# The last differential-attention steps of a hybrid encoder layer: another order of projection, map transposes, key tiles and value products

## The chip, the cores and the metric

The kernel runs on one core of a Trainium2 chip. The metric is the device time in microseconds; three runs of the kernel before gave 828.14, 828.20 and 828.29 us. The engines are named as the profile names them: PE (matmuls and transposes), DVE (vector), ACT (activation functions and copies), POOL, and SP, which issues most of the loads. Each works through its own list of instructions in order and waits on semaphores that the others raise.

## What is computed

One encoder layer on 1024 positions of width 1024: a norm, one wide input projection, two branches over head groups (gated linear attention, then differential attention), an output projection, cross-attention into 256 memory tokens, a last norm. The part that matters here:

```python
# differential attention, per head h and block of 128 queries
s = einsum('bhmqd,bhmkd->bhmqk', qb, kh) * scale     # two maps m, block-causal
p = softmax(where(allowed, s, -inf), axis=-1)
a = p[:, :, 0] - lam * p[:, :, 1]
o = einsum('bhqk,bhke->bhqe', a, vh)                 # then a head norm and a gate
mixed = concatenate([o_gla, o_diff], axis=-1)
x = x + mixed @ w_out
# cross-attention: keys and values of the memory tokens
kv = mem_n @ w_ckv                                   # K is its left half, V its right half
```

## The kernel before

Every float32 product is made of three matmuls of split operands (`_hi` and `_lo`: a rounded part that ACT writes, and the rest that DVE writes), lines 1849 to 1851. So each tile that PE produces and consumes again costs ACT a copy and DVE a subtraction (line 1386) before PE may use it.

The program is one list of stages (`stages()`), which every engine walks in the same order; each engine issues only its own part of a stage. Differential attention has 32 steps i (4 heads of 8 query blocks; step i looks at i % 8 + 1 key blocks of 128). The stages of a step:

- `proja`, `proj` (number 16 + i): the input projection of one block, 24 matmuls of 512 columns; `proja` is its first half where it is split, with other work between the halves.
- `TQK`: queries and keys transposed on PE (L2104), copied by ACT, their low part written by DVE (`qkT_lo`).
- `S`: scores (L2121, L2126). `max`: row maxima by DVE (L1648). `E`: two exponentials by ACT (L1270). `comb`: the two maps combined by DVE (L1656 to L1663); in step 31 in two pieces.
- `T`: the combined map transposed (L1921), in groups of up to four blocks; ACT writes `prT_hi`, DVE `prT_lo`.
- `PV`: the map times the values (L2144, L2146); DVE sums the halves (L1669), ACT squares them (L1101).
- `pvvar`, `pvfin`: variance, POOL's power, and the gated norm (L1675, L991, L1685).

Beside them: `MT`, a stored tile of mixed outputs brought back and transposed on PE (L1921, from `tile_a`); `K` c, a tile of cross-attention keys (24 matmuls of 256 columns), with `Ke` its copy and low part (`ck_hi`, `ck_lo`) into SBUF; `Ka`, the first 18 matmuls of `K` 0; and `("w", n)`, a weight tile split into `w_hi` (ACT) and `w_lo` (DVE), whose slot must have been given up by an older weight tile, and whose stage makes SP load tile n + 4.

Waits that matter below. `PV` of step i waits until the transposed map's low part is there and for a count of `qkT_lo` tiles (`tq_dve`). `MT` waits until all earlier transposed tiles but those of the other bank have been split (`turned_out`). Key tiles 0, 1 and 2 all use bank 0, so each waits for the `ck_lo` of the one before; key tiles 3 and 4 use banks 2 and 3, which belong to the scores, and tile 3 waits for the exponentials of step 31 (`s_act`). Key tile 0 needs the weight tiles 56 to 63.

Of the kernel before, what the change touches and what calls it, by code (L numbers as in the profile page):

```python
# [32 lines left out]
P = 128  # L33
# [77 lines left out]
def stages():  # L111
# [50 lines left out]
    n_turned = 0  # L162
    plan.extend([("S", 0), ("max", 0), ("E", 0), ("comb", 0)])
    plan.extend([("proja", GLA_STEPS + 2), ("TQK", 1), ("proj", GLA_STEPS + 2)])
    for i in range(last):
        plan.append(("S", i + 1))
        plan.append(("max", i + 1))
        plan.extend([("pvvar", i - 1)] if i else [])
        plan.extend(turned_maps(i))
        split = GLA_STEPS + i + 3 in PROJ_SPLIT  # L170
        if i + 2 < DIFF_STEPS and not split:
            plan.append(("TQK", i + 2))
        plan.extend([("pvfin", i - 1)] if i else [])
        plan.extend([("E", i + 1), ("comb", i + 1)])
        plan.extend([("loadm", 0, 0), ("loadm", 1, 0)] if i == DIFF_STEPS - TT - 4 else [])
        if split:
            plan.extend([("proja", GLA_STEPS + i + 3), ("TQK", i + 2)])
        if i + 3 < DIFF_STEPS:
            if i + 3 > DIFF_STEPS - TT and not split:
                plan.append(("proja", GLA_STEPS + i + 3))  # L180
                plan.extend(turned_tile(n_turned))
                n_turned += 1
            plan.append(("proj", GLA_STEPS + i + 3))
            if i + 3 > DIFF_STEPS - TT and split:
                plan.extend(turned_tile(n_turned))
                n_turned += 1
        if i == last - 2:
            plan.extend([("Ka", 0), ("PV", i), ("K", 0), ("Ke", 0)])
        elif i == last - 1:
            plan.extend([("K", 1), ("Ke", 1), ("PV", i)])  # L190
        else:
            plan.append(("PV", i))
    plan.extend([*turned_maps(last), ("pvvar", last - 1), ("K", 2), ("pvfin", last - 1), ("Ke", 2)])
    plan.extend(turned_tile(n_turned))
    n_turned += 1
    plan.extend([("K", 3), ("Ke", 3), *turned_tile(n_turned), ("PV", last), ("pvvar", last), ("pvfin", last)])
    n_turned += 1
    fill = [[("K", c), ("Ke", c)] for c in range(4, 8)] + [[("V", g, m)] for g in range(2) for m in range(MT)]
    for n, more in enumerate(fill):
        plan.extend(more)  # L200
        if n_turned < 2 * TT:
# [116 lines left out]
def with_weights(plan):  # L318
# [20 lines left out]
    for g in range(2, len(use)):  # L339
        before = use[g - 1]  # L340
        early = NW - KT
        for k in range(NK[g]):
            if use[g][0][0] == "X":
                p = use[g][0][1]
                if p == 0:
                    where = ("V", 1, 0) if k < 2 else ("MT", TT - 1, 1)
                else:
                    where = ("X", p - 1, (k // 2 + 1) if p == 1 else (k + 1) // 2)
                after.setdefault(where, []).append(("w", W0[g] + k))
                continue  # L350
            if use[g][0][0] == "Y" and use[g][0][1]:
                p = use[g][0][1]
                if p == 1:
                    where = ("Qe", 1, XH - 1, 0) if k == 0 else (("O", 1, XH - 2, 1) if k < 3 else ("Y", 0, 2))
                else:
                    where = ("Y", *divmod(4 * p + k - min(p + 4, 8), 4))
                after.setdefault(where, []).append(("w", W0[g] + k))
                continue
            if before[0][0] == "X":
                where = ("X", 5, 3) if k < 2 else ("X", 6, k // 2 - 1)  # L360
                after.setdefault(where, []).append(("w", W0[g] + k))
                continue
            where = before[(k + 1) * len(before) // (early + 1)] if k < early and len(before) > 4 else (
                before[min(k // 2, len(before) - 2)] if k < early else before[-1])
            if before[0] == ("K", 0) and k < early:
                where = ("Ke", 1) if k == 0 else ("T", DIFF_STEPS - 1, 1)
            if before[-1] == ("Q", 0, XH - 1, 1) and k >= early:
                where = ("PT", 0, XH - 2, 1)
            if before[0] == ("V", 0, 0) and k < 3:
                where = ("MT", 4, 1)  # L370
            if where == ("proj", GLA_STEPS + DIFF_STEPS - 2):
                where = before[-3]
            elif where == ("proj", GLA_STEPS + DIFF_STEPS - 1):
                where = ("E", DIFF_STEPS - 3) if k == early else ("TQK", DIFF_STEPS - 1)
            elif k >= early and where[0] == "proj" and GLA_STEPS < where[1] < GLA_STEPS + DIFF_STEPS - 1:
                i = where[1] - GLA_STEPS - 3
                where = ("PV", i) if k == early else ("T", i + 1, (i + 1) % TT // 4)
                after.setdefault(where, []).append(("w", W0[g] + k))
                continue
            after.setdefault(behind(where), []).append(("w", W0[g] + k))  # L380
# [65 lines left out]
def late_banks():  # L446
# [10 lines left out]
            bank[("Y", p, t)] = (*PJ_BANKS, 4, 5)[(4 * p + t + 2) % 6]  # L457
    before, held = {}, {}
    for stage in PLAN:
        if stage[0] in ("Ka", "Qa"):  # L460
            stage = (stage[0][0], *stage[1:])
        if stage in PJ and stage not in before:
            before[stage] = held.get(bank[stage])
            held[bank[stage]] = stage
# [47 lines left out]
def build(nc, a, out):  # L512

    with ExitStack() as ctx:
# [1331 lines left out]
        def _(pe):  # L1846
# [77 lines left out]
            for stage in PLAN:  # L1924
# [165 lines left out]
                elif kind == "TQK":  # L2090
# [1 line left out]
                    pe.wait_ge(pj_dve, GLA_STEPS + i + 1)  # L2092
                    wait(pe, tq_dve, i)
                    if TQK_BANK[i] == 1:
                        wait(pe, pv_sum, i - 2)
                    elif i >= 2:
                        turned_out(TR[("T", i - 2, 0)])
                    if i == 0:
# [30 lines left out]
                elif kind == "T":  # L2129
                    i, g = w  # L2130
                    pe.wait_ge(s_dve, i + 1 + (g if i == DIFF_STEPS - 1 else 0))
                    if g:
                        pe.wait_ge(tq_dve, i + 2 if i + 1 < DIFF_STEPS else DIFF_STEPS)
                    turn(stage, [prob[:, 0, cols(b)] for b in range(4 * g, min(4 * g + 4, i % TT + 1))])
                elif kind == "PV":
                    i = w[0]
                    t = i % TT
                    pe.wait_ge(ring_dve, TURN_ACT[("T", i, t // 4)] + 1)
                    wait(pe, pv_sum, i)
                    pe.wait_ge(tq_dve, min(i + 3, DIFF_STEPS))  # L2140

                    for b in range(t + 1):
                        v = (i - t + b) % NV
# [1 line left out]
                                  start=b == 0, stop=False)  # L2145
                        last = pe.matmul(bank1[:, 0:P], prT_lo[:, b, :], dv2[:, v, 0, :], start=False, stop=b == t)  # L2146
                    last.then_inc(pv_pe, 1)
                elif kind == "Ka":
                    job = ("K", *w)
                    pe.wait_ge(pj_dve, GLA_STEPS + DIFF_STEPS)  # L2150
                    project(job, late_bank(job)[:, 0:M], weights(P * w[0]), memory_tokens(slice(0, M)), 0, 6)
                elif kind == "K":
                    open_already = ("Ka", *w) in NTH
                    ps = banks[LATE_BANK[stage]] if open_already else late_bank(stage)
                    if w[0] == 3:
                        pe.wait_ge(s_act, DIFF_STEPS)
                    last = project(stage, ps[:, 0:M], weights(P * (w[0] % 4)), memory_tokens(slice(0, M)),
                                   6 if open_already else 0)
                    signal(last, stage, pr_pe)
                elif kind == "V":  # L2160
                    if LATE_BANK[stage] == 1:
# [98 lines left out]
```

## Time and profile before

| | |
|---|---|
| three runs | 828.14, 828.20, 828.29 us |
| the profiled execution's own time | 828.41 us |
| its span, first to last instruction | 826.7 us |
| granted clock of PE, mean | 0.998 |
| PE, DVE, ACT busy | 99%, 71%, 53% of the span |
| chain that ended last, share of PE | 92% |
| steps of differential attention in the span | about 203 to 488 us |
| the stretch that the change touches | about 399 to 491 us |

The span is 1.7 us shorter than the execution's own time. The busy time of PE counts each matmul until its result is out, while the next one has started already: a 512-column matmul is shown 0.39 us long and the next starts 0.23 us after it. So the busy share hides short pauses; the timeline's starts show them.

### The profile page before, as it was taken

The numbers are of one execution on the slowest core, as the hardware profiler recorded it, in microseconds if no ns is written. First come the engines' busy times: TensorE is split into PE (matmuls) and PEld (weight loads), VectorE is DVE, ScalarE is ACT, GpSimd is POOL, SyncE is SP. The second block draws the span as 40 slices with busy tenths as digits, with TensorE's granted clock in tenths as the row PEclk, the third lists the DMA queues.
The fourth block names the chain that finished last, engine by engine and source line by source line (L and its number), as shares of the span: only waits on it lengthen the run. The fifth ranks groups of instructions, "written<-read, shape, count | busy, mean of one in ns | idle before, by whom it ended". The sixth has DMA issues, their size and how long they took to land.

```text
span 826.7 us, 13231 instructions
## 1 busy us (share of the span) xinstructions
PE 814.4 (99%) x4586; PEld 683.9 (83%) x4586; DVE 586.1 (71%) x1360; ACT 435.6 (53%) x1057; POOL 83.7 (10%) x123
## 2 busy tenths in 40 slices
PE   8999999999999999999999999999999999999996
PEld 7888888888788888888888898888888888888885
DVE  6788677776578678767857878599835464367997
ACT  6875445454455345435545676544645454366443
POOL 3100121210010011111100000010010000001201
PEclk9999999999999999999999999999999999999999
DMA  8321359962233345645412268855422121206945
GB/s 289 115 83 39 102 179 199 186 132 66 62 108 109 88 79 108 130 86 116 102 61 84 61 211 262 265 148 128 134 96 72 45 65 43 85 13 139 215 93 203
DMA packets 70409, 99.21 MB, mean 120 GB/s; under 512 B 6596, under 2 KB 38472, under 8 KB 70344
## 3 DMA queue, kind: packets, MB, share of 16 engines
q1 hardware_dynamic: 52360, 64.29, 24.4%
q0 software_dynamic: 15392, 29.36, 19.8%
q10 hardware_dynamic: 2592, 4.72, 1.8%
q8 instruction: 37, 0.61, 0.3%
q14 instruction: 28, 0.23, 0.1%
HBM read 83.68 MB, written 31.46 MB: 139 GB/s over the span
## 4 chain that ended last, share of the span: by engine, by line
PE 92%; DVE 4%; ACT 1%; DMA 1%; issue 1%; SPq 0%; ACTq 0%
PE bank L1849 14%; PE bank L1851 14%; PE bank L1850 14%; PE banks2to L1849 10%; PE banks2to L1851 10%; PE banks2to L1850 10%; PE banks6to L1921 4%; PE banks2to L2121 3%; PE bank L2144 2%; DVE neg_max L1648 2%; PE bank L2146 1%; PE banks6to L2081 1%; DVE w_lo L1387 1%; PE banks6to L1851 1%; PE banks6to L1849 1%; PE banks6to L1850 1%
## 5 line engine op out<-in xcount | busy, mean ns | idle before, releaser
L1851 PE MATMUL bank<-w_hi,actT_lo 128*128 128x512 f32 x412 | 161.3, 391 | 0.0
L1849 PE MATMUL bank<-w_hi,actT_hi 128*128 128x512 f32 x384 | 156.6, 408 | 0.3
L1850 PE MATMUL bank<-w_lo,actT_hi 128*128 128x512 f32 x384 | 149.9, 390 | 0.0
L1387 DVE SCALAR_TENSOR_TENSOR w_lo<-w_raw,vecs,w_hi 128x512 fp32r<-128x512 f32 x120 | 86.6, 748 | 27.2 <-ACT w_hi L1105 27.1
L1851 PEld LDWEIGHTS bank<-w_hi,actT_lo 128*128 128x128 f32 x412 | 77.4, 188 | 16.9
L1849 PEld LDWEIGHTS bank<-w_hi,actT_hi 128*128 128x128 f32 x384 | 72.2, 188 | 18.0 <-DVE w_lo L1387 1.5
L1105 ACT ACTIVATE w_hi<-w_raw,vecs 128x512 fp32r<-128x512 f32 x120 | 82.5, 719 | 7.7 <-DMA w_raw<-in_w_in 4.1
L1850 PEld LDWEIGHTS bank<-w_lo,actT_hi 128*128 128x128 f32 x384 | 72.4, 189 | 12.6
L991 POOL TENSOR_TENSOR rs_o<-var_o,neg_half 128x1 f32<-128x1 f32 (+1 forms) x48 | 29.0, 604 | 375.6 <-DVE var_o L1675 256.8
L1851 PE MATMUL banks2to<-w_hi,actT_lo 128*128 128x512 f32 x164 | 64.0, 390 | 0.0
L1270 ACT ACTIVATE prob<-banks2to,neg_maxs 128x128 f32<-128x128 f32 (+7 forms) x64 | 46.9, 740 | 15.1 <-DVE neg_maxs L1649 15.0
L1105 ACT ACTIVATE w_hi<-w_raw 128x512 fp32r<-128x512 f32 x56 | 33.8, 627 | 37.5 <-DMA w_raw<-out_sums 13.3
L1648 DVE TENSOR_REDUCE neg_max<-banks2to 128x2 f32<-128x256 f32 (+8 forms) x33 | 43.4, 1316 | 4.6 <-PE banks2to L2126 4.3
L1849 PE MATMUL banks2to<-w_hi,actT_hi 128*128 128x512 f32 x112 | 44.7, 399 | 0.0
L1850 PE MATMUL banks2to<-w_lo,actT_hi 128*128 128x512 f32 x112 | 43.7, 390 | 0.0
L1386 DVE TENSOR_TENSOR w_lo<-w_raw,w_hi 128x512 fp32r<-128x512 f32 x56 | 37.2, 685 | 8.8 <-ACT w_hi L1105 8.8
L1849 PE MATMUL banks2to<-actT_hi,w_hi 128*128 128x512 f32 (+1 forms) x100 | 39.5, 395 | 0.7 <-DVE w_lo L1387 0.7
L1801 DVE TENSOR_REDUCE x_negmax<-banks2to 128x4 f32<-128x1024 f32 x8 | 9.8, 1222 | 41.1 <-PE banks2to L1851 41.1
L1105 ACT ACTIVATE qk_tok<-bank 128x192 f32<-128x192 f32 x27 | 8.9, 331 | 56.9 <-PE bank L1851 56.9
L1851 PE MATMUL banks2to<-actT_hi,w_lo 128*128 128x512 f32 (+1 forms) x100 | 38.3, 383 | 0.0
L1850 PE MATMUL banks2to<-actT_lo,w_hi 128*128 128x512 f32 (+1 forms) x100 | 38.1, 381 | 0.0
L2144 PE MATMUL bank<-dv,prT_hi 128*128 128x256 f32 x144 | 35.3, 325 | 1.4 <-DVE qkT_lo L1386 0.7
(372 smaller groups left out, 2043.9 us busy)
## 6 DMA issues: line engine op xcount, KB each, us to landing
w_raw<-in_w_in SPq DMA_DIRECT2D x56, 256.0 KB, 3.4
out_sums<-in_w_out POOLq DMA_DIRECT2D x11, 1024.0 KB, 10.3
late_sums<-in_w_co POOLq DMA_DIRECT2D x11, 1024.0 KB, 9.3
w_raw<-in_w_ckv SPq DMA_DIRECT2D x32, 256.0 KB, 3.5
w_raw<-in_w_cq SPq DMA_DIRECT2D x32, 256.0 KB, 2.8
stage_in<-in_x SPq DMA_DIRECT2D x8, 512.0 KB, 4.4
tile_a<-mixed ACTq DMA_DIRECT2D x16, 256.0 KB, 3.2
x_res<-in_x SPq DMA_DIRECT2D x8, 512.0 KB, 6.3
```

The costliest lines, as they stand in the source:

```text
L991: pool.tensor_tensor(dst, src, neg_half[:, 0:n], ALU.pow).then_inc(sem_out, 1)
L1105: return act.activation(dst, src, ACT.Copy, scale=scale)
L1270: last = act.activation(prob[:, m, 0:n], wide[:, 2 * m:2 * m + 2, :].rearrange("p j c -> p (j c)")[:, 0:n], ACT.Exp, scale=DQK ** -0.5, bi ...
L1386: return dve.tensor_tensor(dst, src, hi.bitcast(F32), ALU.subtract)
L1387: return dve.scalar_tensor_tensor(dst, src, scale, hi.bitcast(F32), ALU.mult, ALU.subtract)
L1648: then_wait(dve.tensor_reduce(neg_max[:, i % 2, m], both[:, m, :], AX.X, ALU.max, negate=True))
L1849: pe.matmul(dst, l_hi, r_hi, start=start, stop=False)
L1850: pe.matmul(dst, l_hi, r_lo, start=False, stop=False)
L1851: return pe.matmul(dst, l_lo, r_hi, start=False, stop=stop)
L1921: last = pe.transpose(ps[:, cols(j)], src, ident[:, :])
L2121: last = pe.matmul(wide[:, 2 * half + g // 512, 0:keys.stop - g], l[rows, 0, cols(t)], r[rows, 1, keys], start=m == 0, stop=m == 2 and key ...
L2144: pe.matmul(bank1[:, 0:256], prT_hi[:, b, :], dv2[:, v, :, :].rearrange("p a c -> p (a c)"), start=b == 0, stop=False)
```

## The change

The last projection (number 47, step 31) moves from behind the transposes of map 28 to behind those of map 29. Key tile 0 is no longer split in two, and it, the queries and keys of step 31 (`TQK` 31) and key tile 1 stand before the scores of step 31. The value products of step 30 come right behind those scores, the transposes of map 31 behind key tile 3, and the value products of step 31 behind key tile 4. Some weight tiles are split later. Projection 41 is no longer split around its mixed tile (`MT` 0,0), which follows it. Three waits on counts are changed to fit the new order.

```diff
-    for i in range(last):
+    for i in range(last - 2):
...
-        if i + 3 < DIFF_STEPS:
-            if i + 3 > DIFF_STEPS - TT and not split:
+        if i + 3 < last:
+            first_tile = i + 3 == DIFF_STEPS - TT + 1
+            if i + 3 > DIFF_STEPS - TT + 1 and not split:
                 plan.append(("proja", GLA_STEPS + i + 3))
                 plan.extend(turned_tile(n_turned))
                 n_turned += 1
             plan.append(("proj", GLA_STEPS + i + 3))
-            if i + 3 > DIFF_STEPS - TT and split:
+            if first_tile or (i + 3 > DIFF_STEPS - TT and split):
...
-        if i == last - 2:
-            plan.extend([("Ka", 0), ("PV", i), ("K", 0), ("Ke", 0)])
-        elif i == last - 1:
-            plan.extend([("K", 1), ("Ke", 1), ("PV", i)])
-        else:
-            plan.append(("PV", i))
-    plan.extend([*turned_maps(last), ("pvvar", last - 1), ("K", 2), ("pvfin", last - 1), ("Ke", 2)])
+        plan.append(("PV", i))
+    plan.extend([("S", last - 1), ("max", last - 1), ("pvvar", last - 3), *turned_maps(last - 2), ("pvfin", last - 3)])
+    plan.extend([("E", last - 1), ("comb", last - 1), ("proja", GLA_STEPS + last), *turned_tile(n_turned)])
+    n_turned += 1
+    plan.extend([("proj", GLA_STEPS + last), ("PV", last - 2), *turned_maps(last - 1), ("pvvar", last - 2)])
+    plan.extend([("K", 0), ("TQK", last), ("Ke", 0), ("pvfin", last - 2), ("K", 1), ("Ke", 1), ("S", last), ("max", last)])
+    plan.extend([("PV", last - 1), ("E", last), ("K", 2), ("Ke", 2), ("comb", last)])
     plan.extend(turned_tile(n_turned))
     n_turned += 1
-    plan.extend([("K", 3), ("Ke", 3), *turned_tile(n_turned), ("PV", last), ("pvvar", last), ("pvfin", last)])
+    plan.extend([("K", 3), ("Ke", 3), ("pvvar", last - 1), ("pvfin", last - 1), *turned_maps(last), *turned_tile(n_turned)])
     n_turned += 1
-    fill = [[("K", c), ("Ke", c)] for c in range(4, 8)] + [[("V", g, m)] for g in range(2) for m in range(MT)]
+    plan.extend([("K", 4), ("Ke", 4), ("PV", last), ("pvvar", last), ("pvfin", last)])
+    fill = [[("K", c), ("Ke", c)] if c > 4 else [] for c in range(4, 8)] + [[("V", g, m)] for g in range(2) for m in range(MT)]
...
-                where = ("Ke", 1) if k == 0 else ("T", DIFF_STEPS - 1, 1)
+                where = ("Ke", k // 2)
...
             elif where == ("proj", GLA_STEPS + DIFF_STEPS - 1):
-                where = ("E", DIFF_STEPS - 3) if k == early else ("TQK", DIFF_STEPS - 1)
+                after.setdefault(where, []).append(("w", W0[g] + k))
+                continue
...
                     if TQK_BANK[i] == 1:
-                        wait(pe, pv_sum, i - 2)
+                        wait(pe, pv_sum, i - (2 if i < DIFF_STEPS - 1 else 1))
...
-                        pe.wait_ge(tq_dve, i + 2 if i + 1 < DIFF_STEPS else DIFF_STEPS)
+                        pe.wait_ge(tq_dve, i + 2 if i + 2 < DIFF_STEPS else i + 1)
...
-                    pe.wait_ge(tq_dve, min(i + 3, DIFF_STEPS))
+                    pe.wait_ge(tq_dve, i + 3 if i + 3 < DIFF_STEPS else min(i + 2, DIFF_STEPS))
```

The rest of the diff takes `Ka` out of the builder and gives key tile 0 the wait on the last projection's copies. A matmul that stands at line 1849 before stands at line 1852 after, and so on: three lines are added above.

PE, place 1, before: the transposes of map 28 (from `prob`), then the queries and keys of step 30 (from `qk_tok`), then the first half of projection 47.

```order
L1921 MATMUL banks6to<-ident,prob 128x128 [waits mixed_tiles_kept,turned_lo,maps_combined]
L1921 MATMUL banks6to<-ident,prob 128x128 x3
L1921 MATMUL banks6to<-ident,prob 128x128 [waits turned_lo,diff_qkT_lo,maps_combined]
L2104 MATMUL bank<-ident,qk_tok 128x128 [waits pv_summed,diff_qkT_lo,proj_dve]
L2104 MATMUL bank<-ident,qk_tok 128x128
L1849 MATMUL bank<-w_hi,actT_hi 128x512 [waits proj_dve]
L1850 MATMUL bank<-w_lo,actT_hi 128x512
```

PE, place 1, after: the same transposes, then at once the value products of step 28.

```order
L1924 MATMUL banks6to<-ident,prob 128x128 [waits mixed_tiles_kept,turned_lo,maps_combined]
L1924 MATMUL banks6to<-ident,prob 128x128 x3
L1924 MATMUL banks6to<-ident,prob 128x128 [waits turned_lo,diff_qkT_lo,maps_combined]
L2107 MATMUL bank<-ident,qk_tok 128x128 [waits pv_summed,diff_qkT_lo,proj_dve]
L2107 MATMUL bank<-ident,qk_tok 128x128
L2147 MATMUL bank<-dv,prT_hi 128x256 [waits diff_qkT_lo,pv_summed,turned_lo]
L2149 MATMUL bank<-dv,prT_lo 128x128
```

The 24 matmuls of projection 47 and the mixed tile between its halves have left this place; they stand now behind the transposes of map 29.

PE, place 2, before: the end of the transposes of map 30, then key tile 1, the value products of step 30 and the transposes of map 31, then key tile 2.

```order
L1921 MATMUL banks6to<-ident,prob 128x128 x2
L1849 MATMUL bank<-memT_hi,w_hi 128x256 [waits late_proj_done]
...
L2144 MATMUL bank<-dv,prT_hi 128x256 [waits diff_qkT_lo,pv_summed,turned_lo]
...
L1921 MATMUL banks6to<-ident,prob 128x128 [waits turned_lo,maps_combined]
L1921 MATMUL banks6to<-ident,prob 128x128 x3
L1921 MATMUL banks6to<-ident,prob 128x128 [waits turned_lo,diff_qkT_lo,maps_combined]
...
L1849 MATMUL bank<-memT_hi,w_hi 128x256 [waits late_proj_done]
```

PE, place 2, after: the last matmul of key tile 0, the queries and keys of step 31, key tile 1, the scores of step 31, and the value products of step 30.

```order
L1854 MATMUL bank<-memT_hi,w_lo 128x256
L2107 MATMUL bank<-ident,qk_tok 128x128 [waits pv_summed,diff_qkT_lo,proj_dve]
L2107 MATMUL bank<-ident,qk_tok 128x128
L1852 MATMUL bank<-memT_hi,w_hi 128x256 [waits late_proj_done]
...
L2124 MATMUL banks2to<-qkT_hi 128x512 [waits scores_exp,diff_qkT_lo]
...
L2147 MATMUL bank<-dv,prT_hi 128x256 [waits diff_qkT_lo,pv_summed,turned_lo]
```

Between key tile 0 and key tile 1, which use one bank, two transposes are left; the scores of step 31 and the transposes of map 30 stood there before.

ACT, place 3, after: what stands around the exponentials of step 31 (`prob`) and around the first copies of map 31 (`prT_hi`, `x2`). Before, the exponentials stood ahead of the squares (`junk`) of step 30, and `prT_hi` of map 31 ahead of the weight tiles.

```order
L1104 ACTIVATE junk,sq_o<-pv_f 128x128 [waits pv_squares,pv_summed]
L1273 ACTIVATE prob,exp_sum<-banks2to,neg_maxs 128x1024 [waits turned_pe,scores_max]
L1273 ACTIVATE prob,exp_sum<-banks2to,neg_maxs 128x1024 [waits scores_max]
...
L1108 ACTIVATE ck_hi<-banks2to 128x256 [waits w_used]
L1108 ACTIVATE w_hi<-w_raw,vecs 128x512 [waits w_used,weight_loaded1]
L1108 ACTIVATE w_hi<-w_raw,vecs 128x512 [waits w_used,weight_loaded2]
L1108 ACTIVATE w_hi<-w_raw,vecs 128x512 [waits w_used,weight_loaded3]
L1108 ACTIVATE prT_hi<-banks6to 128x512 [waits pv_pe,turned_pe] x2
```

ACT, place 3, before: the same stretch of its list.

```order
L1270 ACTIVATE prob,exp_sum<-banks2to,neg_maxs 128x1024 [waits turned_pe,scores_max]
L1270 ACTIVATE prob,exp_sum<-banks2to,neg_maxs 128x1024 [waits scores_max]
...
L1101 ACTIVATE junk,sq_o<-pv_f 128x128 [waits pv_squares,pv_summed]
L1105 ACTIVATE prT_hi<-banks6to 128x512 [waits pv_pe,turned_pe] x2
...
L1105 ACTIVATE ck_hi<-banks2to 128x256 [waits w_used]
```

The squares of step 30 moved ahead of the exponentials, and the copy of key tile 3 (`ck_hi`, which waits for that tile's last use of its weights) and three weight tiles moved ahead of map 31's copies.

## Rows read from the trace of the kernel before

**Rows 1.** The page's first part: busy us, share of the span, instructions.

```profile
PE 814.4 (99%) x4586; PEld 683.9 (83%) x4586; DVE 586.1 (71%) x1360; ACT 435.6 (53%) x1057; POOL 83.7 (10%) x123
```

**Rows 2.** PE's waits over the span: total us, times, longest us.

```profile
PE bank L2144 <- DVE qkT_lo L1386: 0.7, 1, 0.7
```

**Rows 3.** Timeline at mixed tile 0,0: start, us, engine, instruction, [idle before <-releaser].

```profile
403.03 0.39 PE L1851 MATMUL bank<-w_hi,actT_lo 128*128 128x512 f32 x1
...
403.79 0.63 PE L1921 MATMUL banks6to<-ident,tile_a 128*128 128x128 f32 x4 [0.37 <-DVE qkT_lo L1386]
```

**Rows 4.** Timeline, step 29's scores done, projection 47, value products 28.

```profile
452.21 0.48 PE L1849 MATMUL bank<-w_hi,actT_hi 128*128 128x512 f32 x1
...
454.43 0.41 DVE L1386 TENSOR_TENSOR qkT_lo<-bank,qkT_hi 128x256 fp32r<-128x256 f32 x1
...
458.26 0.28 PE L2144 MATMUL bank<-dv,prT_hi 128*128 128x256 f32 x1
```

**Rows 5.** Timeline: scores 30, map 29, `Ka`, value products 29.

```profile
459.45 0.50 PE L2121 MATMUL banks2to<-qkT_hi 64*128 64x512 f32 x2
...
460.15 0.42 DVE L1669 TENSOR_REDUCE pv_f<-bank 128x128 f32<-128x256 f32 x1
...
460.96 0.85 PE L1921 MATMUL banks6to<-ident,prob 128*128 128x128 f32 x6
...
463.86 0.28 PE L1851 MATMUL bank<-memT_hi,w_lo 128*128 128x256 f32 x1
...
464.30 0.41 DVE L1386 TENSOR_TENSOR qkT_lo<-bank,qkT_hi 128x256 fp32r<-128x256 f32 x1
464.64 1.40 DVE L1387 SCALAR_TENSOR_TENSOR w_lo<-w_raw,vecs,w_hi 128x512 fp32r<-128x512 f32 x2
...
464.86 0.36 PE L2144 MATMUL bank<-dv,prT_hi 128*128 128x256 f32 x1 [0.73 <-DVE qkT_lo L1386]
```

**Rows 6.** Timeline: map 30, maxima and exponentials 31, value products 30.

```profile
468.78 0.96 PE L1921 MATMUL banks6to<-ident,prob 128*128 128x128 f32 x7
...
469.30 1.22 DVE L1648 TENSOR_REDUCE neg_max<-banks2to 128x1 f32<-128x1024 f32 x1
...
472.01 1.15 DVE L1386 TENSOR_TENSOR prT_lo<-banks6to,prT_hi 128x512 fp32r<-128x512 f32 x2
...
472.06 1.11 ACT L1270 ACTIVATE prob<-banks2to,neg_maxs 128x1024 f32<-128x1024 f32 x1
...
472.28 0.27 PE L1851 MATMUL bank<-memT_hi,w_lo 128*128 128x256 f32 x1
...
473.21 0.39 PE L2144 MATMUL bank<-dv,prT_hi 128*128 128x256 f32 x1 [0.66 <-DVE prT_lo L1386]
```

**Rows 7.** Timeline: key tile 2, sum of value products 30, mixed tile 7,0.

```profile
475.73 0.36 PE L1849 MATMUL bank<-memT_hi,w_hi 128*128 128x256 f32 x1
...
476.17 0.42 DVE L1669 TENSOR_REDUCE pv_f<-bank 128x128 f32<-128x256 f32 x1
...
477.54 1.29 DVE L1386 TENSOR_TENSOR prT_lo<-banks6to,prT_hi 128x512 fp32r<-128x512 f32 x2 [0.95 <-ACT prT_hi L1105]
...
478.50 0.28 PE L1851 MATMUL bank<-memT_hi,w_lo 128*128 128x256 f32 x1
...
478.93 0.63 PE L1921 MATMUL banks6to<-ident,tile_a 128*128 128x128 f32 x4 [0.15 <-issue]
```

**Rows 8.** Timeline of DVE: variance of step 30, POOL's power, gated norm.

```profile
481.39 0.15 DVE L1675 SCALAR_TENSOR_TENSOR var_o<-sq_o,eps_sum 128x1 f32<-128x1 f32 x1
482.21 0.35 DVE L1685 SCALAR_TENSOR_TENSOR mix_out<-pv_f,rs_o,gate 128x128 f32<-128x128 f32 x1 [0.66 <-POOL rs_o L991]
```

**Rows 9.** PE's first transposes, and two stretches near the end (busy of PE, PEld, DVE, ACT, POOL; clock).

```profile
1.76 5.38 PE L1929 MATMUL banks6to<-ident 128*128 128x128 f32 x24 [1.76 <-POOL ident L982]
...
820.00:822.00 2.00, 0.46 (x3) 0.04 (x1) 1.38 (x3) 0.78 (x3) 0.36 (x1) 1.00 0.65 262
822.00:824.00 2.00, 0.00 (x0) 0.00 (x0) 0.88 (x2) 1.27 (x2) 0.55 (x1) 0.86 0.62 229
```

More of the change, by code:

```diff
@@ L170, in stages @@
         split = GLA_STEPS + i + 3 in PROJ_SPLIT
-        if i + 2 < DIFF_STEPS and not split:
+        if not split:
             plan.append(("TQK", i + 2))
@@ L459, in late_banks @@
     for stage in PLAN:
-        if stage[0] in ("Ka", "Qa"):
+        if stage[0] == "Qa":
             stage = (stage[0][0], *stage[1:])
@@ L2147, in _ @@
                     last.then_inc(pv_pe, 1)
[L2148 to L2151, printed above, removed]
                 elif kind == "K":
-                    open_already = ("Ka", *w) in NTH
-                    ps = banks[LATE_BANK[stage]] if open_already else late_bank(stage)
+                    ps = late_bank(stage)
+                    if w[0] == 0:
+                        pe.wait_ge(pj_dve, GLA_STEPS + DIFF_STEPS)
                     if w[0] == 3:
                         pe.wait_ge(s_act, DIFF_STEPS)
-                    last = project(stage, ps[:, 0:M], weights(P * (w[0] % 4)), memory_tokens(slice(0, M)),
-                                   6 if open_already else 0)
+                    last = project(stage, ps[:, 0:M], weights(P * (w[0] % 4)), memory_tokens(slice(0, M)))
                     signal(last, stage, pr_pe)
```

## The prediction

> **What bounds the kernel now.** I read the page's busy times first, then PE's waits, then the timeline of the stretch that the change touches. PE is shown busy for 814.4 of 826.7 us, DVE for 71% and ACT for 53% [rows 1], so PE's own list sets the time: what removes a pause of PE shortens the run, what adds one lengthens it, and after the stretch PE has no long pause in which it could catch up. PE's waits show what pauses there are: the longest there is 0.7 us before value products (L2144), behind `qkT_lo` [rows 2], and one as long stands behind `prT_lo` [rows 6].
>
> The timeline shows these pauses longer than the waits do, because a matmul's shown end lies behind the start of the next. The Trainium skill says so too ("Trainium Kernel Development and Optimization", Performance Expectations: matmul busy time misleads since matmuls are pipelined). So I take pauses from start to start, less the usual distance: 0.23 us for 512 columns, 0.12 for 256. That gives 0.76 - 0.23 = 0.53 us before mixed tile 0,0 [rows 3], 1.00 - 0.12 = 0.88 before value products 29 [rows 5], 0.93 - 0.12 = 0.81 before value products 30 [rows 6], and 0.43 - 0.12 = 0.31 before mixed tile 7,0 [rows 7]. Together 2.53 us. By the idle times written in the same rows (0.37, 0.73, 0.66, 0.15) it would be 1.91.
>
> **What the change removes.** All four pauses, I think. Mixed tile 0,0 waited for `qkT_lo` of the step, which now has 12 more matmuls in front of it (2.8 us against a wait of 0.53). The other three places are gone in that form. PE's work is the same; only its order changes. Gain: 2.53 us.
>
> **What it adds.** I walk PE's new list with the old durations, on the clock of the trace before. Four waits come up.
>
> *Place 1: value products 28 behind queries and keys 30.* Half of projection 47 filled this slot from 452.21. The value products need `qkT_lo` of step 30, which DVE writes only after the row maxima, at 454.43, for 0.41 us [rows 4]. From the end of that subtraction to the matmul it frees is 464.86 - 464.71 = 0.15 us [rows 5]. So they start at 454.43 + 0.41 + 0.15 = 454.99, not 452.21: a pause of 2.8 us.
>
> Then come value products 28 (1.19 us, from 458.26 to 459.45), scores 30 (1.51, to 460.96) [rows 4, 5] and the transposes of map 29 (0.115 a block: seven take 0.96 less a tail of 0.27 [rows 6], so six take 0.69), to 458.4. Projection 47 with mixed tile 6,0 inside takes 458.26 - 452.21 = 6.05 us [rows 4], to 464.4. The mixed tile finds the low part of map 29 just ready: maxima of 7 blocks in some 2.1 us (two of 1.22 for 8 [rows 6]) and its `prT_lo` in 1.0 end near 461.1, and it comes at 461.2. Value products 29 take 464.86 to 466.27 by the same 0.235 a block, 1.4 us; map 30 takes 0.8; key tile 0 starts at 466.6. A key tile takes 2.77 + 0.12 = 2.9 us [rows 7], so it ends at 469.5, and queries and keys 31 at 469.75.
>
> *Place 2: key tile 1 behind key tile 0.* Both use bank 0, so key tile 1 needs `ck_lo` of tile 0. On DVE stand before it: the copies of projection 47, over 1.9 us after value products start (458.26 to 460.15 [rows 4, 5]), so at 466.3; three weight tiles at 0.66 (two shown as 1.40, one alone as 0.75 [rows 5]), to 468.3; then the sum of value products 29. From such a sum to the first `prT_lo` behind it, through ACT's squares and copy, is 477.54 - 476.17 = 1.37 us [rows 7]: 469.7. Two `prT_lo` take 1.1 [rows 6], then `qkT_lo` 0.35 and `ck_lo` 0.42: 471.6, and with 0.1 for the semaphore 471.7. Pause: 471.7 - 469.75 = 1.9 us. Before, the scores of step 31 and map 30 lay between these two tiles.
>
> *Place 3: key tile 3 behind the exponentials of step 31.* Key tile 1 ends at 474.6, scores 31 (1.7) at 476.3, value products 30 (7 x 0.235) at 477.9, key tile 2 at 480.8, mixed tile 7,0 (0.4) at 481.2. Key tile 3 uses a bank of the scores. On DVE: `ck_lo` of tile 1 and two weight tiles, behind ACT's copies, until 477.1; the two row maxima, 472.01 - 469.30 = 2.7 us [rows 6], until 479.8; the sum of value products 30. ACT has the squares of that sum ahead of the exponentials, so these start at 480.2 + 0.3 = 480.5, take twice 1.1 us [rows 6] and release PE at 482.9. Pause: 1.7 us. Queued behind them on ACT is the copy of key tile 2, and behind that a weight tile and DVE's `comb` 31, which costs another 0.2 between the two transposed groups of map 31.
>
> *Place 4: mixed tile 0,1 behind map 31.* Key tile 3 ends at 485.8, map 31 at 486.9. Mixed tile 0,1 needs `prT_lo` of the first group of map 31. ACT makes `prT_hi` only after `ck_hi` of tile 3 (from 486.0) and three weight tiles: 488.1. DVE has the same three, to 489.0, then the variance, POOL's power, the gated norm. From variance to norm is 0.82 us [rows 8]; the norm ends at 490.05, `prT_lo` takes 0.69, and with 0.1 PE goes on at 490.85. Pause: 3.95 us. This is the largest term. Before, a whole key tile covered the same chain.
>
> **Sum.** 2.8 + 1.9 + 1.7 + 0.2 + 3.95 = 10.55 us added, 2.53 removed: 8.0 us slower. The profiled execution took 828.41 us (span 826.7 and 1.7 around it), so one like it would take 836.4; the median of the runs is 0.2 lower: 836.2. Bounds of the terms: place 1 between 2.4 (if the 0.15 falls away and PE's list is 0.25 later) and 3.0; place 2 between 1.2 and 2.4 (one weight tile either way); place 3 between 1.0 and 2.4 (the same); place 4 between 3.1 (no wait for POOL) and 4.9 (one row maximum's length more). The gain lies between 1.91 and 2.53. A late start at one place shifts the next chain with it, so the ends don't all come together: 835.0 to 837.6 for this case. DMA is no term: the weight tiles split here are loaded when the fourth before is split, over 3 us ahead.
>
> **Rivals.**
>
> *A: the clock falls in the pauses.* PE's last work ends 0.46 us into the stretch from 820, and the granted clock of 822 to 824 is 0.86, the mean of 1 and 0.5: PE dropped from 2.4 to 1.2 GHz at about 823.4, some 3 us after that [rows 9]. Place 4 leaves PE without work for 3.8 us. In favour: that is longer. Against: pauses of 1 us did nothing. At the lower clock the first 24 transposes took (5.38 - 0.42) / 23 = 0.216 us each [rows 9] against 0.115, so work goes at about half speed, and the stretch at the start lasted over 5 us of work. If it falls near the pause's end and comes back after 3 to 5.5 us, it costs 1.5 to 2.8 us: 838.2.
>
> The Trainium skill's rule ("TensorE: Matmul & The Clock Gate", The HAM clock gate) is that the low clock is the default and activity releases it; the trace agrees with both turns, at the start and the end. By that rule this rival happens once or more.
>
> *B: the first pause pays for the others.* If DVE and ACT use place 1's 2.8 us to get ahead, places 2, 3 and 4 are covered: 828.2 + 2.8 - 2.5 = 828.5, not slower than can be told. It decides at place 3: ACT would have to start the exponentials before 479. Against it: each chain starts from an event of PE (the end of projection 47, of scores 31, of key tile 3), so earlier spare time does not shorten it.
>
> *C: only place 4 is covered*, since the order on DVE leaves the transposed map early: 836.2 - 3.95 = 832.3. Against it stands ACT's list, in which three weight tiles come first.
>
> *D: the new order does as a reader of the diff alone might hope*: no new wait, 828.2 - 2.5 = 825.7. The rows of place 1 speak against it.
>
> **How the numbers follow.** My forecast, 836.2, has 0.57; A 0.32; C 0.06; B 0.03; D 0.02. The range that holds 8 in 10 reaches from the low end of the forecast's case, a little below for its bounds, into most of A: 834.6 to 839.6. What can be told from no change is about 0.2%, or 1.7 us. Slower by more: 0.57 + 0.32 + 0.06 = 0.95; within: 0.03; faster: 0.02.
>
> **What would show it.** In the timeline of after, measured from start to start: no pause before mixed tile 0,0; one of 2.8 us between the two transposes of queries and keys 30 and value products 28, released by `qkT_lo`; one of 1.9 before key tile 1, released by `ck_lo`; one of 1.7 before key tile 3, released by the exponentials; one of about 4 before mixed tile 0,1, released by `prT_lo`. Rival A shows as a granted clock below 1 in slices at 485 to 500 and 256-column matmuls 0.21 us apart. I am wrong if PE's waits add up to less than 5 us more than before, or if a later stage gives time back: the span from key tile 5 to the end should be as long as before.

## The result and the profile after

The changed kernel takes 840.1 us (median of 4 runs, 839.14 to 842.36) against 828.25 before (828.14 to 828.29): 1.0147 times, 95% interval 1.0134 to 1.016. It is slower, as forecast, and by more: 836.2 was forecast, and the range ended at 839.6. Its profiled execution took 840.31 us, 838.6 of them span. (One run each of e3, e10 and e15 below ran at a mean clock of 0.65 to 0.75; these three are left out of every figure here.)

The page's first row, answering [rows 1], has the same 4586 matmuls and a share of PE that is 1% lower:

```profile
PE 818.0 (98%) x4586; PEld 686.8 (82%) x4586; DVE 586.3 (70%) x1360; ACT 435.6 (52%) x1057; POOL 84.2 (10%) x123
```

PE's waits between 399 and 500 us (total, times, longest) answer [rows 2]. These four are all, and they are the four places of the forecast in another order: place 4, 1, 2, 3.

```profile
PE banks6to L1924 <- issue: 3.8, 1, 3.8
PE bank L2147 <- DVE qkT_lo L1389: 2.5, 1, 2.5
PE bank L1852 <- DVE ck_lo L1389: 1.9, 1, 1.9
PE banks2to L1852 <- ACT prob L1273: 1.4, 1, 1.4
```

The timeline of the changed kernel at the four places (start, us, engine, instruction, idle before and its releaser), the row that starts the pause and the one that ends it, with what PE waits for. First places 1 and 2, which answer [rows 4, 5]:

```profile
450.29 1.76 DVE L1651 TENSOR_REDUCE neg_max<-banks2to 128x2 f32<-128x1536 f32 x1 [0.17 <-PE banks2to L2129]
...
450.67 0.38 PE L2107 MATMUL bank<-ident,qk_tok 128*128 128x128 f32 x2
...
453.03 0.41 DVE L1389 TENSOR_TENSOR qkT_lo<-bank,qkT_hi 128x256 fp32r<-128x256 f32 x1
...
453.59 0.35 PE L2147 MATMUL bank<-dv,prT_hi 128*128 128x256 f32 x1 [2.54 <-DVE qkT_lo L1389]
...
469.44 0.38 PE L2107 MATMUL bank<-ident,qk_tok 128*128 128x128 f32 x2
...
471.23 0.41 DVE L1389 TENSOR_TENSOR ck_lo<-bank,ck_hi 128x256 fp32r<-128x256 f32 x1
...
471.70 0.38 PE L1852 MATMUL bank<-memT_hi,w_hi 128*128 128x256 f32 x1 [1.87 <-DVE ck_lo L1389]
```

Then places 3 and 4, which answer [rows 6 to 8]. At place 3 ACT has the first row maxima at 480.12, but stands 3.84 us idle for the sum of value products 30, whose squares come first in its list:

```profile
479.97 0.15 DVE L1652 TENSOR_SCALAR neg_maxs<-neg_max 128x1 f32<-128x1 f32 x1
480.05 1.21 DVE L1651 TENSOR_REDUCE neg_max<-banks2to 128x1 f32<-128x1024 f32 x1
...
481.36 0.41 DVE L1672 TENSOR_REDUCE pv_f<-bank 128x128 f32<-128x256 f32 x1
...
481.81 0.31 ACT L1104 ACTIVATE junk<-pv_f 128x128 bf16<-128x128 f32 x1 [3.84 <-DVE pv_f L1672]
...
484.45 0.38 PE L1852 MATMUL banks2to<-memT_hi,w_hi 128*128 128x256 f32 x1 [1.44 <-ACT prob L1273]
...
487.84 1.94 ACT L1108 ACTIVATE w_hi<-w_raw,vecs 128x512 fp32r<-128x512 f32 x3
...
489.68 1.07 ACT L1108 ACTIVATE prT_hi<-banks6to 128x512 fp32r<-128x512 f32 x2
490.58 0.15 DVE L1678 SCALAR_TENSOR_TENSOR var_o<-sq_o,eps_sum 128x1 f32<-128x1 f32 x1
...
491.39 0.35 DVE L1688 SCALAR_TENSOR_TENSOR mix_out<-pv_f,rs_o,gate 128x128 f32<-128x128 f32 x1 [0.66 <-POOL rs_o L994]
491.66 1.28 DVE L1389 TENSOR_TENSOR prT_lo<-banks6to,prT_hi 128x512 fp32r<-128x512 f32 x2
...
492.44 0.65 PE L1924 MATMUL banks6to<-ident,tile_a 128*128 128x128 f32 x4 [3.81 <-issue]
```

Measured as in the forecast, from start to start less the usual distance, the pauses are 2.7, 2.0, 1.6 and 4.0 us. Place 4's releaser reads "issue" there; that it is `prT_lo` follows from the times, since the first of the two `prT_lo` of 491.66 ends near 492.34 and PE goes on 0.1 us later. What the forecast had not put into its number is in the windows view of the same trace (busy us of PE, PEld, DVE, ACT, POOL, then the granted clock), three stretches and one between them:

```profile
455.40:458.70 3.30, 3.30 (x19) 2.72 (x16) 2.08 (x3) 0.91 (x4) 0.00 (x0) 0.50 0.02 5
459.00:472.00 13.00, 11.13 (x74) 9.91 (x73) 8.95 (x26) 8.37 (x20) 1.09 (x2) 1.00 0.26 86
472.50:475.80 3.30, 3.30 (x18) 3.30 (x17) 0.73 (x2) 0.00 (x0) 0.00 (x0) 0.50 0.60 176
...
493.00:496.30 3.30, 3.30 (x17) 3.30 (x17) 0.00 (x0) 0.69 (x1) 0.00 (x0) 0.50 0.34 117
```

The clock is at 1.2 GHz three times; I call each of these turns a fall. By the clock records these stretches begin at 455.37, 472.44 and 492.92 and last 3.41 us each; they begin 1.8, 0.7 and 0.5 us after PE has resumed work behind places 1, 2 and 4. The timeline shows the second one's start in the distance of 256-column matmuls, 0.12 us and then 0.21:

```profile
472.27 0.28 PE L1853 MATMUL bank<-memT_lo,w_hi 128*128 128x256 f32 x1
472.39 0.36 PE L1854 MATMUL bank<-memT_hi,w_lo 128*128 128x256 f32 x1
472.55 0.42 PE L1852 MATMUL bank<-memT_hi,w_hi 128*128 128x256 f32 x1
472.76 0.42 PE L1853 MATMUL bank<-memT_lo,w_hi 128*128 128x256 f32 x1
```

To add up a trace I use two starts that every kernel has: queries and keys 30, and mixed tile 1,1, behind the last place. For before and after they are

```profile
452.07 0.38 PE L2104 MATMUL bank<-ident,qk_tok 128*128 128x128 f32 x2
487.32 0.27 PE L1921 MATMUL banks6to<-ident,tile_a 128*128 128x128 f32 x1
```

```profile
499.07 0.39 PE L1924 MATMUL banks6to<-ident,tile_a 128*128 128x128 f32 x2
```

so the stretch takes 487.32 - 452.07 = 35.25 us before and 499.07 - 450.67 = 48.40 after (its first start is in the fence of places 1 and 2): 13.15 more. Its start is 1.40 earlier: 0.53 is mixed tile 0,0, and 0.73 was there already at the first 512-column matmul (17.93 against 18.66), where the change does nothing (in e17, the changed kernel again, that matmul starts at 18.29), and from mixed tile 1,1 to the last matmul's start it is 332.8 before and 332.9 after. 13.15 - 1.40 + 0.1 is the span's 11.9 us, and nothing is given back later.

### The profile page after: what moved, and what is told of

It is laid out like the page before. It is cut to its first block, busy times and chain, and to the rows that moved or that the text cites. A ratio compares the mean times of both kernels' runs of the same rounds, so it can differ in the third digit from the quotient of the medians.

```text
span 838.6 us, 13230 instructions
## 1 busy us (share of the span) xinstructions
PE 818.0 (98%) x4586; PEld 686.8 (82%) x4586; DVE 586.3 (70%) x1360; ACT 435.6 (52%) x1057; POOL 84.2 (10%) x123
## 4 chain that ended last, share of the span: by engine, by line
PE 92%; DVE 4%; ACT 1%; issue 1%; DMA 0%; POOL 0%; ACTq 0%; DVEq 0%
PE bank L1852 14%; PE bank L1854 14%; PE bank L1853 14%; PE banks2to L1852 10%; PE banks2to L1854 10%; PE banks2to L1853 10%; PE banks6to L1924 4%; PE banks2to L2124 3%; PE bank L2147 2%; DVE neg_max L1651 1%; DVE w_lo L1390 1%; PE banks6to L2084 1%; PE banks6to L1854 1%; PE banks6to L1852 1%; PE banks6to L1853 1%
```

## The experiments

**Filler in the pauses.** The loop over PE's list puts transposes of the identity into a free PSUM bank ahead of a stage. They do no useful work and are shorter than the pause. e1 fills all four places:

```diff
+            filler = {('PV', 28): (0, 22), ('K', 1): (2, 14), ('K', 3): (6, 11), ('MT', 0, 1): (3, 32)}
             for stage in PLAN:
                 kind, *w = stage
+                for _ in range(filler.get(stage, (0, 0))[1]):
+                    pe.transpose(banks[filler[stage][0]][:, 0:P], ident[:, :], ident[:, :])
```

> The changed kernel with 128x128 transposes of the identity into free PSUM banks at the four pauses: 22 before value products 28, 14 before key tile 1, 11 before key tile 3, 32 before mixed tile 0,1, at 0.115 us each some 2.5, 1.6, 1.3 and 3.7 us of work, less than each pause, so the waits keep their ends. Theory 1 (the pauses cost 8.0 us and the three falls of the granted clock the rest, and the falls come from TensorE standing still in the pauses): clock 1.0 in every stretch, 840.1 - 4.6 = 835.5 us, within 1 us of the forecast's 836.2. Rival 2 (the clock falls for another reason, or the extra time is in the pauses themselves): the falls stay and the time is 840 us. Rival 3 (the filler holds up something else): over 841.

Measured: 836.04 us (835.81 to 837.17), 1.0099 times before (1.0085 to 1.0113), clock at 2.4 GHz from 7.80 to 833.82 us. Theory 1 holds. Its trace has PE's waits from 399 to 500 us nearly filled, and no fall where the changed kernel had one:

```profile
PE bank L1852 <- DVE ck_lo L1389: 0.3, 1, 0.3
PE banks6to L1924 <- issue: 0.3, 1, 0.3
PE banks2to L1852 <- ACT prob L1273: 0.2, 1, 0.2
```

```profile
455.40:458.70 3.30, 3.30 (x27) 2.69 (x26) 2.82 (x3) 1.27 (x4) 0.00 (x0) 1.00 0.00 0
...
472.50:475.80 3.30, 3.30 (x29) 2.62 (x28) 1.32 (x3) 1.61 (x3) 0.00 (x0) 1.00 0.55 173
...
493.00:496.30 3.30, 3.30 (x31) 3.30 (x30) 2.18 (x4) 1.62 (x4) 0.00 (x0) 1.00 0.02 5
```

The stretch between the two starts takes 43.89 us (451.17 to 495.06) against 48.40: the clock's part is 4.5 us in these two traces and 4.1 by the medians. Without it the kernel takes what was forecast.

e2 keeps only the entry of place 4, e7 only that of place 1:

```diff
+            filler = {('MT', 0, 1): (3, 32)}      # e2
+            filler = {('PV', 28): (0, 22)}        # e7
```

> The changed kernel with the filler at place 4 alone (32 transposes before mixed tile 0,1). The four pauses filled gave 836.0 against 840.1, so a fall costs about 4.1 / 3 = 1.4 us. Theory 1 (each fall belongs to the pause ahead of it): falls after places 1 and 2 stay, the one at 492.9 is gone: 840.1 - 1.4 = 838.7 us. Rival 2 (a fall that is prevented at one place comes at another one, place 3 say): three falls and 840. Rival 3 (only the longest pause matters, and the falls near places 1 and 2 were tied to it): 836.

> The changed kernel with the filler at place 1 alone (22 transposes before value products 28). Theory 1: no fall near 455, the ones after place 2 and place 4 stay, 838.7 us. Rival 2 (a fall comes after place 3 instead): 840. Rival 3 (the fall after place 2 needed the one after place 1): one fall, 837.4.

e2 took 837.36 us (836.36 to 837.94; 1.0108, 1.0093 to 1.0124), e7 838.97 (837.77 to 840.07; 1.0127, 1.0113 to 1.0141). In e7's trace the clock fell behind places 2 and 4, as theory 1 has it, and its time is as expected. In e2's it did not fall at all, though places 1 and 2 were open:

```profile
454.50:458.50 4.00, 4.00 (x34) 3.40 (x34) 3.04 (x6) 1.54 (x6) 0.00 (x0) 1.00 0.08 20
471.00:475.00 4.00, 3.99 (x32) 3.72 (x34) 1.96 (x4) 1.04 (x3) 0.00 (x0) 1.00 0.44 143
```

This execution contradicts theory 1 and rival 2. It would fit rival 3, that only the longest pause matters, but e3, where a key tile covers most of place 4, and e15, which has no place 4, each have a fall behind place 1 (both below). So a pause of 2 to 2.7 us is followed by a fall in some executions only. This trace is also a check on the filler itself: its stretch takes 43.91 us with places 1 to 3 open and the clock held, and e1's 43.89 with them filled, so the transposes cost nothing and give back nothing but the clock.

e11 fills places 1 to 3 and leaves 4 open; e12 does so with 16 transposes in place of 32 at place 4.

```diff
+            filler = {('PV', 28): (0, 22), ('K', 1): (2, 14), ('K', 3): (6, 11)}                        # e11
+            filler = {('PV', 28): (0, 22), ('K', 1): (2, 14), ('K', 3): (6, 11), ('MT', 0, 1): (3, 16)} # e12
```

> The changed kernel with the filler at places 1 to 3, and place 4 left open: the pause of 4 us alone. Theory 1: a fall after place 4 in every run, none elsewhere, 836.0 + 1.4 = 837.4 us. Rival 2 (the fall after place 4 needs those before it): 836.0.

> The changed kernel with the filler at places 1 to 3 as before and 16 transposes in place of 32 at place 4, which leave the second half of that pause, some 2.2 us. Theory 1 (a pause of 2 to 3 us makes the clock fall in some runs, as at places 1 and 2, one of 4 us in all): 836.0 in some runs, 837.4 in others. Rival 2 (the length of the pause decides alone, and 2.2 us is too short): 836.0 in all, like all four filled. Rival 3 (what counts is that work is thinner over a longer stretch): 837.4 in all.

e11 took 838.64 us (837.63 to 841.13; 1.0134, 1.0119 to 1.015), e12 838.34 (836.19 to 838.61; 1.0115, 1.0101 to 1.0129). Each trace has one fall, behind place 4. In e12 the pause that was left is this one, and the clock fell 1.4 us after it, at 491.48:

```profile
490.10 0.63 PE L1924 MATMUL banks6to<-ident,tile_a 128*128 128x128 f32 x4 [2.09 <-issue]
```

Three of e12's runs are like e11 and one like e1, so its theory 1 stands for the scatter, though its slower runs are 1 us over the 837.4 expected. e11's theory has the fall right and the time 1.2 us short of the median.

e16 and e17 are second traces of e11 and of the changed kernel, unedited.

> Places 1 to 3 filled and place 4 open once more, for a second trace: its runs took 837.6 us at a mean clock of 0.996 (the one traced, one fall) and 838.4 to 841.1 us at 0.993 and 0.994. Theory 1: the slower ones have two or three stretches of 1.2 GHz behind the one pause. Rival 2: one longer stretch. Rival 3: a fall elsewhere, at a filled place or later.

> The changed kernel once more, for a second trace: its runs took 839.1 to 842.4 us. Theory 1 (place 4's fall comes each time, those of places 1 and 2 in some runs): at least one fall, behind place 4. Rival 2: the same three falls at the same places.

e16 took 838.37 us with the same single fall of 3.41 us (at 490.49). e17 took 839.2 with two: the windows show them behind places 1 and 4, and none behind place 2.

```profile
454.70:458.00 3.30, 3.30 (x19) 2.80 (x17) 1.77 (x5) 0.40 (x2) 0.00 (x0) 0.50 0.09 25
472.00:476.00 4.00, 3.73 (x30) 3.51 (x32) 1.97 (x5) 1.04 (x3) 0.18 (x1) 1.00 0.42 131
...
492.30:495.60 3.30, 3.30 (x18) 3.30 (x17) 0.00 (x0) 0.56 (x1) 0.00 (x0) 0.50 0.34 103
```

**Key tile 4 ahead of mixed tile 0,1** (e3), and the same with places 1 to 3 filled (e8):

```diff
-    plan.extend([... *turned_maps(last), *turned_tile(n_turned)])
-    plan.extend([("K", 4), ("Ke", 4), ("PV", last), ...])
+    plan.extend([... *turned_maps(last)])
+    plan.extend([("K", 4), ("Ke", 4), *turned_tile(n_turned), ("PV", last), ...])
```

> The changed kernel with key tile 4 ahead of mixed tile 0,1, so that 2.9 us of work stand behind map 31. Theory 1 (place 4 is a wait for the low part of map 31, 3.95 us, that a key tile covers, and the third fall of the clock belongs to it): about 1.3 us left there, in pieces, no fall at 492.9, falls 1 and 2 as before; 840.1 - 2.65 - 1.5 = 836.0 us. Rival 2 (the wait moves to value products 31 or to the next tiles in full): 839 to 840. Rival 3 (the third fall stays without the long pause): 837.5.

> The changed kernel with key tile 4 ahead of mixed tile 0,1 and the filler at places 1 to 3. Key tile 4 ahead took 834.9 to 838.6 us by run, by how many falls its run had. Theory 1 (the clock is all that scatters these runs): no fall, all runs within 0.5 us of each other, and 836.0 less the 2.65 us that key tile 4 covers: 833.4 us. Rival 2 (something else scatters them, the reload of mixed tiles say): a spread of 2 us or more stays, 834 to 837.

e3's four other runs took 834.91, 835.07, 837.92 and 838.64 us (1.0104, 1.0086 to 1.0121); the one traced (835.07) has one fall, behind place 1, where its theory 1 expected two, and 1.15 us of pause left at place 4. With the clock held (e8) most of the scatter is gone: 834.36 us, 834.05 to 834.91 (1.0072, 1.0059 to 1.0084), no fall. e8's stretch takes 41.27 us, 2.62 less than e1's, as expected; its median is 1.0 us over the 833.4 expected. So one key tile covers most of place 4, and the clock makes most of e3's spread of 3.7 us.

**ScalarE's order at place 3** (e13), with places 1, 2 and 4 filled:

```diff
-    plan.extend([("PV", last - 1), ("E", last), ("K", 2), ("Ke", 2), ("comb", last)])
+    plan.extend([("E", last), ("PV", last - 1), ("K", 2), ("Ke", 2), ("comb", last)])
```

> The changed kernel with the exponentials of step 31 ahead of the squares of value products 30 in ScalarE's list, and the filler at places 1, 2 and 4. Theory 1 (place 3 is that order: the exponentials wait for row maxima and also for the squares of a sum that VectorE makes only behind both maxima): the pause before key tile 3 falls from 1.6 us to under 0.2, nothing else grows, 836.0 - 1.75 = 834.3 us. Rival 2 (the maxima alone set it): 836.0.

835.05 us (834.66 to 835.29; 1.008, 1.0067 to 1.0094). Key tile 3 follows mixed tile 7,0 without a wait, and the stretch between the two starts takes 42.25 us against e1's 43.89: 1.64 less, the whole pause. The medians differ by 1.0 only. Place 3 was the order of two entries in ACT's list.

**Place 1 alone.** e5 is the kernel before with one part of the change, projection 41 whole and mixed tile 0,0 behind it. e10 adds to e5 value products 28 ahead of projection 47; e15 repeats it, e14 fills its pause.

```diff
+            first_tile = i + 3 == DIFF_STEPS - TT + 1                        # e5
-            if i + 3 > DIFF_STEPS - TT and not split:
+            if i + 3 > DIFF_STEPS - TT and not split and not first_tile:
...
-            if i + 3 > DIFF_STEPS - TT and split:
+            if first_tile or (i + 3 > DIFF_STEPS - TT and split):
```

```diff
+                plan.extend([("PV", i)] if i == last - 3 else [])            # e10
                 plan.append(("proja", GLA_STEPS + i + 3))
...
-        else:
+        elif i != last - 3:
             plan.append(("PV", i))
```

> The kernel before with one part of the change alone: projection 41 whole and mixed tile 0,0 behind it, all else as before. Theory 1 (that part alone takes away the 0.53 us pause before mixed tile 0,0 and nothing else): 828.2 - 0.5 = 827.7 us, clock 1.0 until the end. Rival 2 (DVE or ACT catch the pause up a step later): 828.2.

> The kernel with projection 41 whole (827.7 us) and one more edit: value products 28 ahead of projection 47, so that nothing stands between them and queries and keys 30. Theory 1 (place 1 costs its pause, and nothing behind it gives it back, since each later chain starts from an event of TensorE): a pause of 2.7 us, the later ones as before, 827.7 + 2.8 = 830.5 us, with one fall of the clock in some runs, 831.9. Rival B of the forecast (VectorE and ScalarE use the pause to get ahead, and the pauses of 0.9, 0.8 and 0.3 us behind it go): 828.5 us.

> The kernel with place 1 alone (projection 41 whole, value products 28 ahead of projection 47) and the filler of 22 transposes in that pause. Theory 1 (the pause costs 2.8 us that nothing gives back, and the clock the rest of what place 1 alone took, 831.8 to 833.6 us in undisturbed runs): 830.5 us, all runs within 0.5. Rival B (the pause is paid back): under 829.

> Place 1 alone once more, for a trace. Theory 1: a pause of 2.7 us before value products 28, pauses of 0.9, 0.8 and 0.3 us behind it as before, and one stretch of 1.2 GHz or more behind the pause; 831.8 to 833.6 us. Rival B: the later pauses are gone.

e5: 827.67 us (827.47 to 827.82; 0.9995, 0.9986 to 1.0004), the 0.5 us expected, within what can be told from no change. e10's four other runs took 831.83 to 833.55, e15's 830.57 to 832.2; e14 831.06 (830.44 to 831.32; 1.0032, 1.0019 to 1.0044), 0.6 over what e10 and e14 expected. PE's waits in e15's trace from 440 to 500 us: the two on `qkT_lo` are place 1 (2.5) and the old one before value products 29, the third is the old one before value products 30.

```profile
PE bank L2146 <- DVE qkT_lo L1388: 3.4, 2, 2.5
PE bank L2146 <- DVE prT_lo L1388: 0.7, 1, 0.7
```

No later pause has gone, so rival B is wrong: earlier slack does not shorten a chain that starts from an event of PE. Between the two starts e14 takes 38.09 us and e15 39.67, against 35.25 before: 2.8 for the pause and 1.6 for the one fall that e15's trace has.

**Two other orders.** e6 and e9 start from e5 and give the stages from value products 28 to key tile 5 as a list. Both put queries and keys 31 ahead of map 29's transposes; their tails are

```diff
+    ('K', 3), ..., ('PV', 31), ('MT', 7, 0), ..., ('K', 4), ('MT', 0, 1), ..., ('K', 5), ('MT', 1, 1), ..., ('MT', 2, 1), ...   # e6
+    ('K', 3), ..., ('MT', 7, 0), ..., ('PV', 31), ..., ('MT', 0, 1), ..., ('K', 4), ..., ('MT', 1, 1), ..., ('K', 5), ..., ('MT', 2, 1), ...   # e9
```

> The kernel before with that part, and from value products 28 on an order of its own: queries and keys 31 ahead of map 29's transposes, value products 31 ahead of mixed tile 7,0, key tile 4 ahead of mixed tile 0,1. Walked with the durations of the trace before: pauses of 0.7 us before value products 29 and 0.45 before value products 30, none before mixed tile 7,0, 0.9 us less than before in all, and 0.53 at projection 41. Theory 1: 828.2 - 1.4 = 826.8 us. Rival 2 (the walk misses copies of ACT or weight tiles that come late in this order): 828 to 830.

> As the run of the kernel before with an order of its own, but with mixed tile 7,0 between key tile 3 and value products 31, and mixed tile 0,1 behind those, so that every mixed tile's reload, which took 4.1 us from issue to landing in that run and was waited for three times (1.7 us), has a key tile or more before it is used. Theory 1 (the reload was what the walk missed): 829.0 - 1.7 = 827.3, and without the pauses that the walk still has up to 826.8 us. Rival 2: over 828, another wait comes.

e6: 828.97 us (828.51 to 829.73; 1.0011, 1.0002 to 1.002), rival 2's range and 2.2 us over theory 1. PE's waits from 445 to 500 us name what the walk had left out, the reload of a mixed tile:

```profile
PE banks6to L1933 <- DMA tile_a<-mixed: 1.7, 3, 0.9
```

e9, with work between each reload and its use: 827.1 us (826.65 to 827.92), 0.9984 times before (0.9975 to 0.9993). That is theory 1's 826.8 to 827.3. It is faster than both kernels, than before by 0.16%: the interval excludes no change, but the size is below the 0.2% that the forecast named. No wait on a reload is left.

## Why the prediction was right or wrong

**The four places: right**, in place, releaser and size. Forecast 2.8, 1.9, 1.7 and 3.95 us, measured 2.7, 2.0, 1.6 and 4.0. The pause before mixed tile 0,0 is gone, and e5 shows that part alone (0.5). With the clock held, the stretch takes 43.89 - 35.25 = 8.6 us more, less the 0.53 won before it: 8.1 against the forecast's 8.0. That e1's median, 836.04 us, also comes within 0.2 of 836.2 is closer than these runs allow one to ask: between traces the part behind mixed tile 1,1 alone, where these kernels do not differ, takes 332.8 to 333.8 us.

**The step that failed is rival A**, the clock. The forecast's sum has no term for it, and the range went as far as one fall: "It costs 1.5 to 2.8 us: 838.2" is the price of place 4's alone. The price of a fall was about right, at its low end: the clock came back after 3.41 us, where the forecast took 3 to 5.5. The number of falls was not. The changed kernel's trace has three, worth 4.5 us. The traces of kernels with open places, with the time between the two starts, less e1's 43.89 (for e15 e14's 38.09, for e3 e8's 41.27), over the falls:

| trace | open places | falls behind | stretch, us | a fall, us |
|---|---|---|---|---|
| changed | 1 to 4 | 1, 2, 4 | 48.40 | 1.50 |
| e17 | 1 to 4 | 1, 4 | 46.97 | 1.54 |
| e7 | 2 to 4 | 2, 4 | 47.01 | 1.56 |
| e11 | 4 | 4 | 45.48 | 1.59 |
| e16 | 4 | 4 | 45.46 | 1.57 |
| e12 | half of 4 | 4 | 45.46 | 1.57 |
| e15 | 1 | 1 | 39.67 | 1.58 |
| e3 | 1 to 3, 1.15 us of 4 | 1 | 42.80 | 1.53 |
| e2 | 1 to 3 | none | 43.91 | |

With 256-column matmuls 0.21 us apart in place of 0.12, PE does in 3.41 us what else takes about 1.9: an estimate of 1.5 us lost, as measured, since each fall began after PE was at work again. The pause of 4.0 us was followed by a fall in 5 traces of 5 where it was open, the one of 2.7 in 4 of 5, the one of 2.0 in 2 of 5, the one of 1.6 in none of 5, and no pause of before's size (1.0 us at most) had one. So the error was in the argument "against: pauses of 1 us did nothing", from which I gave places 1 and 2, of 2.8 and 1.9 us, no fall at all, and which held rival A's chance at 0.32. The rows of before held pauses of 1 us without a fall and a fall after the last work [rows 9], and nothing between; 1.9 and 2.8 us lay between, and I took them to be like the 1 us. The rule of the Trainium skill that the forecast cites ("TensorE: Matmul & The Clock Gate", The HAM clock gate) is that the low clock is the default and activity releases it. The falls behind the pauses agree with it; as cited, it doesn't say which pause is too short for a fall, and for that there are only the counts above.

**By medians** places 1 to 3 open cost 837.36 - 836.04 = 1.3 us over all filled, place 4 open 838.64 - 836.04 = 2.6, all open 4.1. The 2.6 is 1.0 more than the one fall of 1.6 us in e11's and e16's traces, and no run shows what the rest is; medians of four runs, each kernel's taken at another time, scatter by about that much. So place 4 cost its 4.0 us of pause and 1.6 for the fall, 5.6 by the traces.

**Rivals B, C and D**: no pause was paid back (e15), none was covered, and all four came. The later part is as long as before, as forecast.

**What stays open.** Three of e11's runs have a mean clock of 0.993 or 0.994 (the traced run, with one fall, has 0.996), and 838.4 to 841.1 us. More falls would explain it, but no trace of such a run is on record: the second trace of that kernel (e16) has one fall and decides between none of its three theories. Of the 841.1 us only 837.4 are span, so 2 us of that run lie outside the program's instructions and aren't the clock's. Why an equal pause has a fall in one execution and none in another isn't shown either: in each trace the pause itself was the same within 0.03 us.

## What to carry to other kernels

Price a pause of TensorE twice: its length, and the fall of the clock that may follow. Here a fall cost 1.5 to 1.6 us more and came behind pauses of 2.0, 2.7 and 4.0 us in 2, 4 and 5 traces of 5; a kernel with several such pauses shows it first in a spread of its runs. To part the two, fill the pause with transposes of the identity into a free bank: what the time falls by is the clock's. Walking each engine's list with the durations of the old trace gave waits within some 0.1 us, but the walk must have the DMA reloads in it as well, or it prefers an order that waits for them.

## What the runs showed of the hardware

- The fall comes after the pause: in the twelve cases traced, 0.1 to 1.8 us after PE is at work again (455.37 against 453.59 in the changed kernel, 454.18 against 454.10 in e15), and each lasts 3.41 us, in which PE is busy all the time (3.30 of 3.30 us in each window shown).
- Half a filler was not half a cure: with 16 transposes in place 4's pause and 2.26 us left, the clock still fell in the trace, and the median (838.34) is that of the open pause (838.64).
- A reload of a mixed tile takes 2.6 to 5.1 us from issue to landing in e6 (median 4.1 of 7).
